# Merged rows transposed by VectorE in 32x32 blocks and regrouped by sixteen SBUF transfers, in place of identity products on TensorE

## The reference

```python
ya = jnp.einsum('bsc,cd->bsd', oa * jax.nn.silu(ga), w_o_a[l])      # 1024 -> 2048
yb = jnp.einsum('bsc,cd->bsd', ob * jax.nn.silu(gb), w_o_b[l])      # 1024 -> 2048
merged = jax.nn.sigmoid(ma) * ya + jax.nn.sigmoid(mb) * yb
x = x + jnp.einsum('bsd,de->bse', merged, w_out[l])                 # 2048 -> 2048
```

## Time and profile before

| what | value |
|---|---|
| time, median of 3 runs | 797.82 us (797.64 to 798.22) |
| span of the profiled execution | 796.4 us |
| PE busy | 792.7 us of 796.4 |
| DVE busy | 481.5 us (60%) |
| ACT busy | 418.4 us (53%) |
| chain that ended last | PE 97% |
| granted TensorE clock | full in every slice |

### The profile page before, as it was taken

One profiled execution on the slowest core, in us unless ns is written; L12 is line 12 of the kernel. 1 busy time (PEld: TensorE's weight loads), 2 busy tenths in 40 slices (PEclk: granted clock), 3 DMA queues, 4 the chain that ended last, 5 costly groups with the idle time before them and its releaser, 6 DMA issues.

```text
span 796.4 us, 10773 instructions
## 1 busy us (share of the span) xinstructions
PE 792.7 (100%) x3810; PEld 667.3 (84%) x3810; DVE 481.5 (60%) x663; ACT 418.4 (53%) x670; POOL 46.8 (6%) x70
## 2 busy tenths in 40 slices
PE   9999999999999999999999999999999999999998
PEld 9998888888888888888888888888888888888887
DVE  7677766666677554668656455555455566665453
ACT  7574556665555454556465554555575444443431
POOL 4341000000000000000000000000000000000000
PEclk9999999999999999999999999999999999999999
DMA  9986665666666565666655665655665855555563
GB/s 316 313 264 198 186 187 168 183 199 180 199 187 187 171 194 162 196 189 193 177 154 173 166 176 161 185 160 172 173 185 182 293 195 184 185 194 189 187 194 122
DMA packets 81082, 152.92 MB, mean 192 GB/s; under 512 B 5136, under 2 KB 12944, under 8 KB 80784
## 3 DMA queue, kind: packets, MB, share of 16 engines
q1 hardware_dynamic: 80752, 152.06, 62.8%
q10 hardware_dynamic: 288, 0.30, 0.1%
HBM read 150.25 MB, written 2.10 MB: 191 GB/s over the span
## 4 chain that ended last, share of the span: by engine, by line
PE 97%; ACT 1%; DMA 1%; SPq 0%; issue 0%; DVE 0%; ACTq 0%
PE ps L527 30%; PE ps L529 30%; PE ps L528 29%; PE ps L538 2%; PE ps L569 1%; PE ps L580 1%; DMA raw<-in_w_in 1%; PE ps L638 0%; PE ps L749 0%; PE ps L748 0%; PE ps L747 0%; PE ps L646 0%; ACT L938 0%; ACT L832 0%; ACT g L832 0%; PE ps L626 0%
## 5 line engine op out<-in xcount | busy, mean ns | idle before, releaser
L1068 DVE TENSOR_TENSOR lo<-raw,hi 128x1024 fp32r<-128x1024 f32 (+2 forms) x279 | 335.2, 1204 | 290.2 <-ACT hi L819 288.4
L819 ACT ACTIVATE hi<-raw 128x1024 fp32r<-128x1024 f32 (+2 forms) x277 | 287.1, 1040 | 337.4 <-PE ps L529 323.8
L527 PE MATMUL ps<-hi,hT_hi 128*128 128x512 f32 (+2 forms) x936 | 364.3, 389 | 0.0
L529 PE MATMUL ps<-hi,hT_lo 128*128 128x512 f32 (+2 forms) x936 | 361.1, 386 | 0.0
L528 PE MATMUL ps<-lo,hT_hi 128*128 128x512 f32 (+2 forms) x936 | 360.8, 385 | 0.0
L529 PEld LDWEIGHTS ps<-hi,hT_lo 128*128 128x128 f32 x936 | 175.7, 188 | 35.1
L528 PEld LDWEIGHTS ps<-lo,hT_hi 128*128 128x128 f32 x936 | 175.8, 188 | 32.9
L527 PEld LDWEIGHTS ps<-hi,hT_hi 128*128 128x128 f32 x936 | 175.7, 188 | 33.0
L527 PE MATMUL ps<-hi,ogT_hi 128*128 128x512 f32 x128 | 50.1, 391 | 0.0
L529 PE MATMUL ps<-hi,ogT_lo 128*128 128x512 f32 x128 | 49.8, 389 | 0.0
L528 PE MATMUL ps<-lo,ogT_hi 128*128 128x512 f32 x128 | 49.8, 389 | 0.0
(11 more groups left out here) (167 smaller groups left out, 484.5 us busy)
## 6 DMA issues: line engine op xcount, KB each, us to landing
raw<-in_w_in SPq DMA_DIRECT2D x192, 512.0 KB, 3.8
raw<-in_w_out SPq DMA_DIRECT2D x32, 512.0 KB, 4.3
raw<-in_w_o_a SPq DMA_DIRECT2D x16, 512.0 KB, 3.7
raw<-in_w_o_b SPq DMA_DIRECT2D x16, 512.0 KB, 3.6
raw<-in_w_in SPq DMA_DIRECT2D x13, 384.0 KB, 5.3
raw<-in_w_in SPq DMA_DIRECT2D x8, 336.0 KB, 5.3
x_own<-in_x SPq DMA_DIRECT2D x4, 512.0 KB, 6.4
g<-in_x SPq DMA_DIRECT2D x1, 2048.0 KB, 10.3
```

What stands on the lines that cost most here:

```text
L527: mm(o, a_hi, w_hi[:, j], start=first and j == 0, stop=False)
L529: ins = mm(o, a_lo, w_hi[:, j], start=False, stop=j == 1 and last)
L819: activation(hi[:, slot, :, 0:width], raw[:, slot, :, 0:width], ACT.Copy).then_inc(hi_ready, 1)
L1068: tt(lo[:, slot, :, 0:width], raw[:, slot, :, 0:width], hi[:, slot, :, 0:width].bitcast(F32), ALU.subtract).then_inc(lo_ready, 1)
```

## The change

The identity products of the merged rows go. VectorE now transposes `stage` in blocks of 32 by 32 numbers into `swapped`, one instruction for the whole 128x1024 tile. The block that lies on partitions 32q to 32q+31 and belongs to feature rows 32c to 32c+31 has then to go to partitions 32c to 32c+31: sixteen DMA transfers on the SP queue, each of 32 partitions by 256 numbers (32 KB), move the blocks from `swapped` to `roped`. They are issued in two lots of eight, behind the first and behind the second weight load of a chunk. ScalarE copies from `roped` to `hT_hi` and VectorE subtracts to `hT_lo`, both from SBUF and not from PSUM, one instruction for each half of the tokens, behind the `hi` and the `lo` of the fourth ring step (i == 4) instead of at steps 2 and 3. The SP loops over chunks of the tail are written out.

```diff
+            def bring_turned(n, q):
+                sp.wait_ge(merged_turned, n + 1)
+                for c in range(P // BLOCK):
+                    src, to = (t[at * BLOCK:(at + 1) * BLOCK, :, :].rearrange("j r n -> j (r n)")[:, block * S:(block + 1) * S]
+                               for t, at, block in ((swapped, q, c), (roped, c, q)))
+                    sp.dma_start(to, src).then_inc(turned_back, 16)
+
+            def move_merged(n, i):
+                if n >= 0 and i < 2:
+                    bring_turned(n, 2 * i)
+                    bring_turned(n, 2 * i + 1)
...
-            def merged_steps(n):
-
-                pe.wait_ge(merged, n + 1)
-                pe.wait_ge(split_lo, n * 2 + 16)
-                for half in range(2):
-                    transpose_step(lambda b, r: stage_r[:, r, (2 * half + b) * P:(2 * half + b + 1) * P], T0 + half)
...
-                    if n == 0 and i == 2:
-                        merged_steps(3)
                     if i == 0:
                         pe.wait_ge(tail_out, 6 + n + 1)
-                    if n == 0 and i in (0, 6, 7):
-                        pe.wait_ge(split_lo, {0: 22, 6: 23, 7: 24}[i])
+                    if n == 0 and i in (0, 4, 6):
+                        pe.wait_ge(split_lo, {0: 20, 4: 22, 6: 24}[i])
...
-            def merged_hi(n, half):
-                t = n * 2 + half
-                split_hi_step(t + 16, hT_hi, t * 2, T0 + half)
+            def merged_hi(n):
+
+                act.wait_ge(turned_back, 256 * n + 256)
+                for r in range(RT):
+                    to = hT_hi[:, bass.ds(n * 4, 4), r * P:(r + 1) * P]
+                    activation(by_blocks(to), columns_of(roped, r), ACT.Copy).then_inc(split_hi, 1)
...
-                dve.wait_ge(split_T, n * 2 + 8)
                 tt(stage[:, :, :], a_part, b_part, ALU.add).then_inc(merged, 1)
...
+                dve.wait_ge(merged, n + 1)
+                nc.vector.transpose(swapped[:, :, :].rearrange("p r n -> p (r n)"),
+                                    blocks_of(stage)).then_inc(merged_turned, 1)
+
+            def merged_lo(n):
+
+                for r in range(RT):
+                    dve.wait_ge(split_hi, n * 2 + (17 + r))
+                    to, rounded = (t[:, bass.ds(n * 4, 4), r * P:(r + 1) * P] for t in (hT_lo, hT_hi))
+                    tt(by_blocks(to), columns_of(roped, r), by_blocks(rounded).bitcast(F32),
+                       ALU.subtract).then_inc(split_lo, 1)
```

More of the change, by code:

```diff
@@ L46 @@
 CW = 512
+BLOCK = 32
 X_CUTS = (0, 1, 2, 4, 6, 8, 10, 12, 14, 16)
@@ L220, in build_layer, with blocks_of, columns_of, by_blocks @@
         swapped_r = sb("swapped_r", [P, RT, CW], F32R, at=swapped_at)
+        def blocks_of(t):
+            return t[:, :, :].rearrange("p r (b c i) -> p c (r b) i", c=P // BLOCK, i=BLOCK)
+        def columns_of(t, r):
+            return t[:, :, :].rearrange("p r n -> p (r n)").rearrange("p (q r b i) -> p r b q i", q=P // BLOCK, r=RT,
+                                                                      i=BLOCK)[:, r]
+        def by_blocks(t):
+            return t.rearrange("p b (q i) -> p b q i", i=BLOCK)
         QB_COLS = 3 * P
@@ L322, in build_layer @@
         gates_ready = sem("gates_ready")
-        merged = sem("merged")
+        merged, merged_turned, turned_back = sem("merged"), sem("merged_turned"), sem("turned_back")
         last_pieces, rest_added = sem("last_pieces"), sem("rest_added")
@@ L401, in load_projections @@
                         load(i, n * 8 + (U_O + 4 * b + i), weights, 2 * i, n * CW)
+                        move_merged(n - 2, 4 * b + i)
+            def bring_turned(n, q):
[8 more added lines that the diff above has]
+                    bring_turned(n, 2 * i + 1)
             load_projections(0)
@@ L405, in _ @@
             sp.dma_start(g[:, :, :], x_rows).then_inc(res_landed, 16)
-            with sp.Fori(1, 4) as n:
+            for n in range(1, 4):
                 load_projections(n)
-            with sp.Fori(0, 4) as n:
+            for n in range(4):
                 for i in range(CK):
                     load(i % RING, n * CK + (U_W + i), w_out, 2 * i, n * CW)
+                    if n < 2:
+                        move_merged(n + 2, i)
             for n in range(3):
@@ L729, in projections @@
                         first = isinstance(n, int)
-                        if not first and branch == 0 and i == 2:
-                            merged_steps(n - 1)
                         if i == 0 and first:
@@ L1024, in _ @@
                 for i in range(8):
-                    if i in (2, 3):
-                        merged_hi(n - 1, i - 2)
+                    if i == 4:
+                        merged_hi(n - 1)
                     tail_hi_ahead(n, i)
@@ L1335, in gate_b_and_merge @@
                 dve.wait_ge(tail_out, n * 2 + 2)
-                dve.wait_ge(split_T, n * 2 + 8)
                 tt(stage[:, :, :], a_part, b_part, ALU.add).then_inc(merged, 1)
-            def merged_lo(n, half):
-                t = n * 2 + half
-                split_lo_step(t + 16, hT_lo, hT_hi, t * 2, T0 + half)
+                dve.wait_ge(merged, n + 1)
[7 more added lines that the diff above has]
+                       ALU.subtract).then_inc(split_lo, 1)
             def tail_lo_ahead(n, i):
@@ L1355, in _ @@
                         gate_b_and_merge(n - 1)
-                    if i in (2, 3):
-                        merged_lo(n - 1, i - 2)
                     if i == 4:
                         gate_a(n)
+                        merged_lo(n - 1)
                     tail_lo_ahead(n, i)
@@ L1365, in _ @@
                         gate_b_and_merge(3)
-                    if n == 4 and i in (2, 3):
-                        merged_lo(3, i - 2)
+                    if n == 4 and i == 4:
+                        merged_lo(3)
                     if n >= 5 and i == 0:
```

## The result

The changed kernel takes 811.35 us (median of 4 runs, 811.12 to 811.73) where the kernel before takes 797.73 beside it: a ratio of 1.0171, 95% interval 1.0156 to 1.0185. It is slower by 13.6 us. The forecast was 797.9 and the range ended at 803.0, so this lies well outside.

A forecast was written before the change was run, and what follows sets the result against it. PE's matmul stream was taken to bound the kernel: 796.4 us span less 3.0 for removed products plus 3.1 for one stall gives 796.5, plus 1.4 from span to median, 797.9 us. The range over the cases was 795.4 to 803.0.

The forecast's parts named there:

- What bounds it: Whole kernel: as long as PE's stream of matmuls, PE busy for 792.7 of 796.4 us.
- what the removed products are worth: PE's stream in the four merged chunks: eight identity products cost 0.75 us each time, 3.0 us in all.
- The shape of the chain: Chunk 3's merged rows: transpose, seventeen issues on SP, landing, two copies, two remainders, then PE, which stalls 3.09 us.
- the last landing: Last small transfer of chunk 3: lands 1.9 us after its issue, from 1.7 up to 3.9.
- the issue interval: SP queue: 0.46 us per 32 KB transfer, bounds 0.39 and 0.52; counted 17 times, 7.82 us.
- The half-way load: SP queue: the load of U_W+9 between the two lots of eight transfers, one of the 17 issues taken at 0.46 us.
- L: Sum of all errors along the chain, in us; all low bounds together give -1.9, the issue's upper end 1.0.
- the prediction's own price: Net change in us: 0.1 + L + 3 x max(0, L - 0.33), the other three chunks having 0.33 us of margin.
- The first rival: Blocks land over 0.33 us late, delaying the next chunk's first `hi`; +3.9 us, 801.7, at L = 1.2; chance 0.28.
- The weight loads: Loads on SP behind the small transfers: up to 3.5 us late, costed at nothing, with two units of slack behind.
- the half clock: PE behind a 3 us gap: one or two units at 1.2 GHz, +2.8 to +5.5 us; a rival, chance 0.12.

The follow-up runs named there:

- no_moves: The changed kernel without its sixty-four small transfers, ScalarE and VectorE reading the transposed tile in place (output wrong): 795.16 us, 0.9963 of the kernel before.
- issue_probe: The kernel before plus sixteen unused transfers of four kinds on the idle SP queue: issues take 0.59 to 0.60 us within SBUF, 0.42 from HBM.
- filled: The changed kernel with products of zeros on PE in front of the waits where it had gaps: 811.07 us, 1.0166 of the kernel before.
- idle_moves: The kernel before, identity products kept, plus sixty-four unused transfers of the same shape at the same places of the SP queue: 799.45 us, 1.0017.
- later_step: The changed kernel with the merged rows' copies and subtractions of chunks 0 to 2 moved behind step 7 of the chunk: 814.66 us, 1.0211 of the kernel before.
- one_lot: The changed kernel with all sixteen transfers in one lot on SP ahead of the load of unit 8: 809.81 us, 1.0152 of the kernel before.
- two_queues: The changed kernel with its sixteen transfers shared, eight on SP and eight on ScalarE's queue: 797.71 us, 0.9999 of the kernel before.
- two_ahead: The changed kernel with eight transfers on ScalarE's queue and eight on SP in one lot ahead of the load of unit 8: 796.98 us, 0.9992.
- half_count: The changed kernel with eight transfers of 64 KB per chunk in place of sixteen of 32 KB (output wrong): 796.73 us, 0.9985 of the kernel before.

## Why the prediction was wrong, by its own steps

**What bounds it, and what the removed products are worth**: right, or nearly. 3.0 us were said, no_moves shows 2.7 in the medians and the span of its profile is 3.1 shorter.

**The shape of the chain** was right from end to end, and most terms were: the transpose 1.25 against 1.23, the last landing 1.88 against 1.9, the copies 0.62, the two remainders 1.29 against 1.4. From the sum into `stage` to the load of unit U_W+8 it is 3.64 us against 3.78.

**The step that failed is the issue interval.** The prediction took 0.46 us for a 32 KB transfer, from rows of transfers out of HBM, with 0.52 as the upper bound, and named it as the term that counts 17 times. Measured are 0.591 for the issue and 0.634 from one to the next, 10.37 us for the 17 (718.63 to 729.00) where 7.82 were summed. The half-way load, also taken at 0.46, is slowed with them. That alone is L = 2.55, and by the prediction's own price 0.1 + 2.55 + 3 x 2.22 = +9.3. The first rival, every chunk stalls, was therefore what happened; it had a chance of 0.28 and a price of +3.9, because L stood only at 1.2 in it. The upper bound came from the nearest rows by size, but all of them had one end in HBM; issue_probe shows that this is the property that matters and that size is not.

**How far the corrected sum goes.** The formula's price for the three chunks is right in kind. With L = 2.55 the first matmul of a chunk comes 21.43 + 2.55 = 23.98 us behind that of the chunk before, a loop that PE only waits for; measured are 24.51, 24.08 and 24.28, and filled shows that this loop has a pace of its own. Up to unit 6, from the same start, the changed kernel is 5.35 + 5.38 = 10.7 behind the kernel before, against 9.3 by the formula. The 1.4 between them is not taken apart. Two terms of it the rows show: the 1.71 of one issue in the first lot, and the sum into `stage`, which in the w_out chunk starts 4.43 behind the first matmul (714.99) where the prediction had 3.69, as VectorE must first make the remainders that the stall held up.

**Two terms were left out.** The weight loads were costed at nothing behind two units of slack. idle_moves puts them at 1.5 us when nothing else is late, and later_step and one_lot show that they are a second path to PE once the first is shortened. In the changed kernel itself the runs give them no share of their own. And the half clock was set as a rival beside the stalls, where it comes with them: 2.8 us behind the last gap. Then 10.7 + 2.8, less the 0.4 by which the changed kernel was ahead at the start, are the 13.1 of the span. The medians differ by 13.6: the profiled execution of the kernel before was one of its slower ones, for in all of its executions with a span on record the whole time is 1.7 to 1.9 over it, which makes this one about 798.2. The prediction took 1.4 for this, an error of 0.4.

**The landing** of 1.9 us was right for the last transfer in the changed kernel, which follows its load by 5 us. It was 3.3 in two_queues and 3.1 for the last two of two_ahead, where loads are issued close by.

**What stays open** is how the 7.6 us that the three chunks take over PE's stream divide between the two paths:

| kernel | three chunks, us | six units, us |
|---|---|---|
| before | 67.52 | 17.08 |
| no_moves, no transfers | 65.28 | 16.32 |
| idle_moves, late loads only | 68.83 | 17.04 |
| changed | 72.87 | 22.46 |
| later_step, rows' wait moved | 69.94 | 28.22 |
| one_lot, rows sooner and loads later | 73.14 | 21.33 |

With the rows' wait out of the way 4.7 of the 7.6 stay; with idle transfers beside the identity products only 1.3 come. Why late loads cost more in later_step than in idle_moves was not tried.

## What to carry to other kernels

A transfer has a price on the queue that issues it, here the same for 1 KB and for 128 KB; where the queue also feeds a ring of loads, sixteen small ones are ten microseconds during which hardly anything else starts. Before putting work there, take the issue time from a row of transfers with the same two ends that follow each other, multiply by the count, and follow both what waits for the last of them and what stands behind them. When two late paths meet in one engine, moving one tells little: take the cause away, here the count or the queue, and use the old way for the one piece whose reader is near.

## What the runs showed of the hardware

- In a row of its like an issue on SP takes 0.59 to 0.60 us with both ends in SBUF, for 32 and for 128 partitions, for 1 KB and for 128 KB, and 0.42 from HBM. The first issue from HBM behind one within SBUF takes 0.58, and one within SBUF behind a load 0.51. SP's and ScalarE's queue issue beside each other, four transfers in 2.5 to 2.9 us in place of 2.4.
- The granted clock fell to half behind gaps of PE: behind 4.3, 2.6 and 2.2 us of rest in the changed kernel, and behind 1.9 in the profile of two_queues, where five of eleven executions have the lower clock. It stayed full behind 0.4 in the changed kernel, 1.3 in half_count and 1.6 in the profile of two_ahead. The Trainium skill, TensorE: Matmul & The Clock Gate, under Why this matters for your kernels, warns of idle gaps in mid-kernel; the traces agree.
- VectorE transposes 128x1024 float32 numbers in 32x32 blocks in 1.245 us, as fast as it adds them.
- GpSimd's queue sends a small transfer each 0.49 to 0.51 us, and it lands after 4.3.
